# A mixture-of-experts layer: two experts' products summed in PSUM by one set of 0/1 matmuls, in two places of a turn, and 8 KB rows of down weights

## The reference

```python
# t: 576 x 1024 (normalised tokens); 4 groups x 8 experts; gates: 2 of 32 are nonzero for a token
for g in range(N_GROUPS):
    e = slice(g * EXPERTS_PER_GROUP, (g + 1) * EXPERTS_PER_GROUP)
    hg = jnp.einsum('td,edf->tef', t, w_gate[e])       # 1024 -> 512
    hu = jnp.einsum('td,edf->tef', t, w_up[e])
    h = jax.nn.silu(hg) * hu * gates[:, g, :, None]
    y = y + jnp.einsum('tef,efd->td', h, w_down[e])    # 512 -> 1024
x = rmsnorm(x + y)
```

## Time and profile before

| | us |
|---|---|
| median of 3 runs | 769.97 |
| the three runs | 769.97, 767.77, 771.99 |
| the profiled execution | 769.66 |
| its span | 767.8 |
| PE / DVE / ACT busy | 710.1 / 400.0 / 110.3 |
| DMA, mean over the span | 299 GB/s |

### The profile page before, as it was taken

How to read it: one execution, slowest core, us unless ns; L and a number is a source line. 1 busy time by engine, 2 the same in 40 slices (tenths; PEclk the granted TensorE clock), 3 DMA queues, 4 the chain that set the end, 5 groups by cost and what they waited for, 6 DMA issues and landing times.

```text
span 767.8 us, 9080 instructions
## 1 busy us (share of the span) xinstructions
PE 710.1 (92%) x3792; PEld 356.2 (46%) x3792; DVE 400.0 (52%) x697; ACT 110.3 (14%) x202; POOL 39.5 (5%) x47
## 2 busy tenths in 40 slices
PE   7999999999889999999999999999999999999691
PEld 5999999778644333333333333333333333332220
DVE  5464166424354555545555455554555545555447
ACT  6322242203200000000000000000000000000004
POOL 1000000000020001000010000000000000000000
PEclk9999999999788999999999999999999999999997
DMA  9921400583576999999999999999999999996003
GB/s 289 322 89 47 175 1 1 222 337 128 187 312 241 391 399 399 402 402 387 409 408 402 399 409 405 410 398 404 382 407 411 410 396 398 404 415 251 1 0 124
DMA packets 53421, 229.84 MB, mean 299 GB/s; under 512 B 7844, under 2 KB 15029, under 8 KB 36995
## 3 DMA queue, kind: packets, MB, share of 16 engines
q1 hardware_dynamic: 50819, 224.52, 74.8%
q0 software_dynamic: 2560, 4.73, 1.6%
HBM read 228.03 MB, written 4.85 MB: 303 GB/s over the span
## 4 chain that ended last, share of the span: by engine, by line
PE 79%; DVE 14%; ACT 3%; DMA 2%; issue 1%; SPq 1%; DVEq 0%; POOLq 0%
PE ps L1447 31%; PE ps L1467 15%; PE ps L1284 12%; PE ps L1477 8%; PE ps L1355 7%; DVE x_sb L788 6%; DVE xT L1125 2%; DVE hexp L788 2%; ACT silu_g L750 2%; DVE hexT L1133 1%; DMA x_sb<-in_x_prompt 1%; PE ps L1381 1%; DMA xg<-hn_rows,idx 1%; PE ps L1248 1%; PE ps L1250 1%
## 5 line engine op out<-in xcount | busy, mean ns | idle before, releaser
L788 DVE TENSOR_TENSOR x_sb<-ps,x_sb 128x512 f32<-128x512 f32 (+1 forms) x330 | 211.5, 682 | 136.1 <-PE ps L1477 103.3
L1447 PE MATMUL ps<-w,xT 128*64 128x512 f32 x1024 | 246.6, 605 | 1.2 <-DVE xT L1125 1.2
L1467 PE MATMUL ps<-wd,hexT 128*64 128x512 f32 x512 | 118.3, 605 | 24.9 <-DVE hexT L1133 24.9
L1447 PEld LDWEIGHTS ps<-w,xT 128*64 128x64 f32 x1024 | 65.7, 137 | 130.5 <-issue 127.6
L1477 PE MATMUL ps<-y_hi,home 64*128 64x512 f32 (+1 forms) x320 | 78.0, 484 | 8.7 <-DVE x_sb L788 5.6
L1467 PEld LDWEIGHTS ps<-wd,hexT 128*64 128x64 f32 x512 | 34.3, 138 | 95.7 <-issue 55.8
L794 DVE SCALAR_TENSOR_TENSOR y_lo<-ps,gate_of,y_hi 128x512 fp32r<-128x512 f32 x32 | 24.0, 751 | 94.7 <-ACT y_hi L754 94.7
L1477 PEld LDWEIGHTS ps<-y_hi,home 64*128 64x128 f32 (+1 forms) x320 | 28.1, 172 | 97.6 <-DVE x_sb L788 57.7
L1477 PE MATMUL ps<-y_lo,home 64*128 64x512 f32 (+1 forms) x320 | 63.5, 393 | 0.0
L750 ACT ACTIVATE silu_g<-ps 128x256 f32<-128x256 f32 x32 | 12.3, 383 | 297.8 <-PE ps L1447 297.8
L558 POOL DMA_INDIRECT xg<-hn_rows,idx x32 | 32.2, 1007 | 429.0 <-PE ps L1437 424.4
(11 more groups left out here) (205 smaller groups left out, 586.7 us busy)
## 6 DMA issues: line engine op xcount, KB each, us to landing
w<-in_moe_w_gate SPq DMA_DIRECT2D x64, 1024.0 KB, 8.3
w<-in_moe_w_up SPq DMA_DIRECT2D x64, 1024.0 KB, 10.7
wd<-in_moe_w_down SPq DMA_DIRECT2D x64, 1024.0 KB, 8.6
wo<-in_w_out SPq DMA_DIRECT2D x2, 2048.0 KB, 10.8
x_sb<-in_x_prompt SPq DMA_DIRECT2D x4, 512.0 KB, 9.1
hn_rows<-hn2p SPq DMA_DIRECT2D x4, 512.0 KB, 2.8
out<-x_sb SPq DMA_DIRECT2D x4, 512.0 KB, 2.6
wi_v<-in_w_in SPq DMA_DIRECT2D x4, 384.0 KB, 8.2
```

Of the source, the lines that this page charges most:

```text
L788: return nc.vector.tensor_tensor(out, a, b, op)
L1447: last = mm(ps[64 * h:64 * h + 64, 1, :], lhs, w1[s][:, :, k, h * (F // 2):(h + 1) * (F // 2)], start=(k == 0), stop=(k == KD - 1))
L1467: last = mm(ps[64 * h:64 * h + 64, 3, :], lhs, wd[s][:, c, h * 512:(h + 1) * 512], start=(c == 0), stop=(c == F // P - 1))
```

## The change

It has four parts.

1. **Pairs.** The homes of experts 2p and 2p+1 are one set: five homes for two experts, each of which sums y_hi and y_lo of both in PSUM (8 matmuls instead of 4), and five adds for two experts instead of ten. A third set of y_hi, y_lo and home takes the room of a routing table.
2. **Places.** `gate_up` is no longer broken up. Pair p's homes stand in turns 2p+2 and 2p+3: homes 0 and 1 after `transpose_x` and home 2 after `transpose_act` of the even turn, homes 3 and 4 after `transpose_x` of the odd turn. VectorE copies hexT ahead of xT. The last pair's homes, after turn 31, have four pairs of banks in place of two.
3. **Overflow.** Nothing is flushed ahead of `blocks_past`: turn 30's `transpose_x` and `work` are in turn 29, and its own xT stays where it is if blocks follow (they use `xT_past`).
4. **Down rows.** The rows of the down weights are dealt to partitions in twos, 8 KB of DRAM each; the transposes of the activation take every second column so that they match. SyncE issues the down weights of slot 2 when the first gather has landed, and not when it is issued.

TensorE's list, before: the `down` of turn 27 and most of turn 28's `gate_up`. L1467 is `down`, L1447 `gate_up`, L1477 the homes; x4 is four alike in a row.

The hexT copy stands behind one add, as before, and no longer behind the xT copy. The core of the diff:

```diff
             gate_v = w_gate[0].rearrange("e (p k) f -> p e (k f)", p=P)
             up_v = w_up[0].rearrange("e (p k) f -> p e (k f)", p=P)
-            down_v = w_down[0].rearrange("e (c p) d -> p e c d", p=P)
+            down_v = w_down[0].rearrange("e (h p r) d -> p e h (r d)", p=P, r=2)
             def load_down(e, s, landed=None):
                 for half in range(2):
-                    c = slice(half * (F // P // 2), (half + 1) * (F // P // 2))
-                    sp.dma_start(wd[s][:, c, :].rearrange("p (o c) d -> p o c d", o=1),
-                                 down_v[:, bass.ds(e, 1), c, :]).then_inc(landed or wd_in[s], 16)
+                    sp.dma_start(wd[s][:, 2 * half:2 * half + 2, :].rearrange("p (o c) d -> p o (c d)", o=1),
+                                 down_v[:, bass.ds(e, 1), half, :]).then_inc(landed or wd_in[s], 16)
...
-            sp.wait_ge(idc_seen, 2)
+            sp.wait_ge(xg_in[0], 16)
             load_down(2, 2)
...
-                pool.sem_inc(idc_seen, 1)
                 gather(xg[:, s, :], idx[:, n:n + 1], xg_in[s])
...
-            def turn(n, adds, more=True):
-                if adds:
-                    for j in range(3):
-                        add_first(n - 1, j)
+            def turn(n):
+
+                p, second = n // 2 - 1, n % 2
                 work_h(main, n)
-                if more:
+                if p >= 0:
+                    add_pair(p, 3 * second)
+                work_hT(main, n)
+                if n < NE - 1:
                     work(main, n + 1)
-                if adds:
-                    add_first(n - 1, 3)
-                work_hT(main, n)
-                if adds:
-                    add_first(n - 1, 4)
+                if p >= 0:
+                    for j in ((1, 2), (4,))[second]:
+                        add_pair(p, j)
...
-                    last = nc.tensor.transpose(ps[:, 2, c * P:(c + 1) * P], hexp[:, c * P:(c + 1) * P], ident)
+                    last = nc.tensor.transpose(ps[:, 2, c * P:(c + 1) * P], hexp[:, c:F // 2:2], ident)
...
+                steps = [(buf, y) for buf in bufs for y in (y_hi, y_lo)]
+                for i, (buf, y) in enumerate(steps):
                     for h in range(2):
                         r = slice(64 * h, 64 * h + 64)
+                        last = mm(ps[0:n, bank + h, :], home[buf][r, t], y[buf][r, :], start=(i == 0),
+                                  stop=(i == len(steps) - 1))
                 last.then_inc(S["home_ps"], 1)
 
-            def home_first(n, j):
-                turn = n * NT + j
+            def home_pair(p, j):
+                q = p * NT + j
                 if j == 0:
-                    pe.wait_ge(main["lo_ready"], n + 1)
-                if turn >= 2:
-                    pe.wait_ge(main["added"], turn - 1)
-                send_home(main, n % 2, j, turn)
-
-            def turn(n, homes, more=True):
+                    pe.wait_ge(main["lo_ready"], 2 * p + 2)
+                if q >= 2:
+                    seen = q - 1 if p < NPAIR - 1 else min(q - 1, p * NT) if j < 4 else p * NT + 1
+                    pe.wait_ge(main["added"], seen)
+                send_home(main, (2 * p % 3, (2 * p + 1) % 3), j, LAST_BANKS[j] if p == NPAIR - 1 else bank_of(q))
+
...
-                gate_up(main, n, s, w1_in[s], need, between)
-                if more:
+                gate_up(main, n, s, w1_in[s], need)
+                if n < NE - 1:
                     transpose_x(main, (n + 1) % NSLOT, xg_in[(n + 1) % NSLOT], 16 * ((n + 1) // NSLOT + 1))
-                if homes:
-                    home_first(n - 1, 3)
+                if p >= 0:
+                    for j in ((0, 1), (3, 4))[second]:
+                        home_pair(p, j)
                 transpose_act(main, n)
-                if homes:
-                    home_first(n - 1, 4)
+                if p >= 0 and not second:
+                    home_pair(p, 2)
...
             transpose_x(main, 0, xg_in[0], 16)
             stay_warm(WARM[3], x_sb[:, 0, :])
             for n in range(LAST):
-                turn(n, n > 0, n < LAST - 1)
-            for j in range(NT):
-                home_first(LAST - 1, j)
+                turn(n)
...
             blocks_past(pe, before_past, block_past, after_past)
-            transpose_x(main, LAST % NSLOT, xg_in[LAST % NSLOT], 16 * (LAST // NSLOT + 1))
             for n in range(LAST, NE):
-                turn(n, n > LAST, n < NE - 1)
+                turn(n)
             for j in range(NT):
-                home_first(NE - 1, j)
+                home_pair(NPAIR - 1, j)
```

More of the change, by code:

```diff
@@ L265, in build @@
     back = region(routing_at, where["zp"])
-    y_hi = back("y_hi", [P, 2, D // 2], F32R)
-    y_lo = back("y_lo", [P, 2, D // 2], F32R)
-    home = back("home", [P, 2, T], F32R)
+    y_hi = [back(f"y_hi{b}", [P, D // 2], F32R) for b in range(2)]
+    y_lo = [back(f"y_lo{b}", [P, D // 2], F32R) for b in range(2)]
+    home = [back(f"home{b}", [P, T], F32R) for b in range(2)]
     p1 = region(where["zp"], pool_end)
@@ L285, in build @@
     onehot_p = p3("onehot_p", [P, 3, NT * 2, NOV], F32R)
+    third = region(where["onehot_s"], pool_end)
+    y_hi.append(third("y_hi2", [P, D // 2], F32R))
+    y_lo.append(third("y_lo2", [P, D // 2], F32R))
+    home.append(third("home2", [P, T], F32R))
+    xT_past = nc.alloc_sbuf_tensor_at("xT_past", [P, KD // 2, P], F32, offset=where["xg"])
     choices = memb[:].rearrange("p t k e -> p (t k) e")
@@ L753, in high @@
                 act.wait_ge(S["dn_ps"], done)
-                nc.scalar.activation(y_hi[:, buf, :], ps[:, 3, :], ACT.Copy, scale=gate).then_inc(S["hi_ready"], 1)
+                nc.scalar.activation(y_hi[buf][:], ps[:, 3, :], ACT.Copy, scale=gate).then_inc(S["hi_ready"], 1)
             def block_first(n):
@@ L1135, in low, with add @@
             def low(S, n, buf, row, gate):
-                ts(home[:, buf, :], row_ids[:], row, None, ALU.is_equal)
+                ts(home[buf][:], row_ids[:], row, None, ALU.is_equal)
                 dve.wait_ge(S["hi_ready"], n + 1)
-                stt(y_lo[:, buf, :], ps[:, 3, :], gate, y_hi[:, buf, :].bitcast(F32), ALU.mult,
+                stt(y_lo[buf][:], ps[:, 3, :], gate, y_hi[buf][:].bitcast(F32), ALU.mult,
                     ALU.subtract).then_inc(S["lo_ready"], 1)
-            def add(S, n, j, turn, seen):
+            def add(S, j, bank, seen):
                 m = TOK[j]
@@ L1206, in _ @@
             for j in range(NT):
[L1207 removed]
+                add_pair(NPAIR - 1, j)
                 if j:
@@ L1438, in transpose_x, with gate_up @@
                 last.then_inc(S["xT_ps"], 1)
-            def gate_up(S, n, s, landed, need, between=nothing):
+            def gate_up(S, n, s, landed, need, xT=xT):
                 pe.wait_ge(S["xT_ready"], n + 1)
@@ L1452, in gate_up @@
                         last.then_inc(S["gu_ps"], 1)
-                    between(k)
             def transpose_act(S, n):
@@ L1469, in down, with send_home @@
                 last.then_inc(S["dn_ps"], 1)
-            def send_home(S, buf, j, turn):
+            def send_home(S, bufs, j, bank):
                 n, t = TOK[j], slice(j * P, j * P + TOK[j])
-                for part, y in enumerate((y_hi, y_lo)):
+                steps = [(buf, y) for buf in bufs for y in (y_hi, y_lo)]
+                for i, (buf, y) in enumerate(steps):
                     for h in range(2):
                         r = slice(64 * h, 64 * h + 64)
-                        last = mm(ps[0:n, 4 + 2 * (turn % 2) + h, :], home[r, buf, t], y[r, buf, :], start=(part == 0),
-                                  stop=(part == 1))
+                        last = mm(ps[0:n, bank + h, :], home[buf][r, t], y[buf][r, :], start=(i == 0),
+                                  stop=(i == len(steps) - 1))
@@ L1512, in _ @@
             for n in range(LAST):
-                turn(n, n > 0, n < LAST - 1)
-            for j in range(NT):
-                home_first(LAST - 1, j)
+                turn(n)
             def before_past():
                 pe.sem_inc(spill["dn_ps"], 1)
-                pe.wait_ge(main["added"], LAST * NT)
+                pe.wait_ge(main["added"], (LAST // 2 - 1) * NT)
+                pe.wait_ge(main["xT_ready"], LAST + 1)
+                pe.wait_ge(main["lo_ready"], LAST)
             def block_past(b):
                 transpose_x(spill, SPARE, xg_past, 16 * b + 16)
-                gate_up(spill, b, SPARE, w1_past, 32 * b + 32)
+                gate_up(spill, b, SPARE, w1_past, 32 * b + 32, xT_past)
                 transpose_act(spill, b)
```

50 lines of the change are left out of this document (24 added, 26 removed).

## The result

| | before | after |
|---|---|---|
| median, us | 770.74 (4 runs) | 711.46 (4 runs) |
| the runs, us | 767.77 to 771.99 | 709.0 to 715.88 |
| the profiled execution, its span | 769.66, 767.8 | 710.51, 708.5 |

The ratio of the times is 0.9242, with a 95% interval of 0.9188 to 0.9297. The change makes the kernel 7.6% faster; 716 us was forecast, with a range of 706 to 730.

What follows compares the result with a forecast made beforehand. TensorE's order was taken to bound the experts, the weight stream shortly behind. The later of two paths, TensorE's 713.1 and the stream's 708.8, plus 1 us for late pieces gave 714.1 of span; forecast 716 us, range 706 to 730.

Steps and rivals of the forecast that it cites:

- the crossing: The weight stream starts two turns ahead, loses 0.9 us a turn and meets TensorE only in the last turns.
- late pieces: 1 us added to the span for weight pieces that come late where TensorE's path and the stream's cross.
- The turns: TensorE's expert turns: even ones take 14.84 us and odd ones 14.14, against 16.03 before.
- The flush: Homes ahead of the overflow test and the restart cost 8.46 us before turn 30; gain 8, with 0.5 left for the test.
- The start: First gather without down weights beside it: gain between nothing and 1.8 us, taken as 1.0; turn 1 starts at 246.0.
- The stream's path: Weight pieces at 2.50 us, 15.35 a turn with the gather, end the span at 708.8 us.
- The rows of the down weights: Down rows of 8 KB instead of 4 KB: no gain counted; a 5% slower 4 KB piece would make 7 us.
- The strided read: Activation's two transposes: nothing taken, covered by the add in odd turns; in even ones 0.44 in 15 turns, 7 us.
- Turn 30 and the tail: End of the experts: turn 30, now with homes, gives back 2.4 us and the tail 0.5.
- The stream decides at 2.56 a piece: Rival: at 2.56 us or more a piece the weight stream sets the end, 720 to 730 us; chance 0.18.
- Homes dearer: Rival: home steps in their new places cost 0.335 us each, 20 us over 29 turns, giving 736 us; chance 0.10.
- The clock falls: Rival: waits for weights lower TensorE's clock in the second half of gate_up, giving 816 us; slower by the clock, chance 0.02.

Runs made afterwards that it cites:

- the kernel without homes: The changed kernel with the homes and adds of all pairs but the last left out: 708.69 us, ratio 0.9184.
- The kernel without homes and with 4 KB rows: The changed kernel with homes and adds of all pairs but the last left out and down weights in 4 KB rows: 713.80 us, ratio 0.9254.
- the odd turn's 6 us: The changed kernel with home 4 behind transpose_act and hexT copied ahead of home 3's add in odd turns: 710.72 us, ratio 0.9219.

## Why the prediction was right

The beat, the places of the waits and the crossing came out as worked out; the time was 4.5 us too high, of 5.6 in the span. The 5.6 are 2.6 at the start of turn 1, 2.0 in turns 2 to 29, 0.5 for the overflow test and 1.0 set aside for late pieces, less 0.5 for turns 30 and 31, which took longer. Point by point:

- *The turns.* 14.84 and 14.14 were forecast, 14.75 and 14.10 measured. Over turns 2 to 29 that is 2.0 us. `gate_up` unbroken is 6.96 (270.48 to the `transpose_x` at 277.44) and not 7.02; the rest is right within 0.03. An even turn is 0.65 longer than an odd one, 0.70 by the forecast. But I called this the price of the wait of home 2 for home 0's add, and that was a wrong name for it: the wait is less than 0.1, as the transposes of the activation end with the add, and the price is home 2's own 1.13 ahead of `down` less the 0.52 of an odd turn's wait for hexT. The sum had these terms right.
- *The flush* went with no gap left; the 0.5 for the overflow test was not needed. Undoing it alone costs 5.5, the 9.3 of the flush less what two turns without homes give back.
- *The start* is the term that was mis-sized most. "The gain is between nothing and 1.8 ... I take 1.0." It was 3.7. The bound was wrong: I took 5.3, the landing of a piece of 1 MB, as the least that a gather could take. The gathers issued in 216 to 220.6 in the kernel after answer:

```profile
DMA to landing us min/median/max: 3.1/3.4/3.7
```

  A gather moves 0.15 MB and should not have been bounded by a piece seven times its size. What held TensorE then is the routing's matmuls, not the gather. Undoing the edit costs 4.3 in the time.
- *The stream's path.* Forecast 708.8 of span, measured 707.5 in the kernel without homes. That near hit is two errors that cancel: the stream started 2.7 earlier than I had it, at 243.46, and a turn took 15.46 in place of 15.35, 3.1 over 28 turns. Of the 1.7 that is left, 0.9 is turn 31, which has no homes in that kernel; 0.8 stays open.
- *The rows of the down weights.* "I count nothing and leave both to the range" was the one step that failed by its reasoning. I wrote that a slower 4 KB piece would be "7 us of a path that doesn't decide". Rows of 4 KB cost 3% of a piece, 4.3 us of the stream's path, and this is enough for it to decide: 3.3 us of the time. The mean of a burst of mixed pieces over 15 us could not show 3%.
- *The strided read* costs 0.07 in a turn whose hexT copy waits for the transposes (14.10 against 14.03 with rows of 4 KB), and nothing in the even turn. I had it the other way round: home 2 covers it in the even turn, and in the odd turn the add ends just ahead of the transposes and covers all but this.
- *Turn 30 and the tail.* Turn 30 took 15.2 (14.84 forecast), with the first wait for weights in it. The tail gave back the 0.5 that was forecast.

The rivals. *The stream decides at 2.56 a piece:* it did not; by the turns of 15.46, less 0.35 for a gather, a piece takes 2.52 with 8 KB rows, and by those of 15.61 a mean one 2.54 with 4 KB down rows, which already push the time up. I wrote that the Trainium skill speaks against the change. Its 408.7 GB/s ("DMA: Bandwidth & Descriptors", section "SWDGE vs HWDGE vs iDMA") is given for rows of 4 KiB. The change takes the down weights, the only ones in such rows, out of them, so the figure does not speak against it. Nor does it fall in this case: by a piece of 2.50 + 0.077 an estimate for a stream of 4 KB rows here is 407 GB/s, while 8 KB rows move 419 to 420. *Homes dearer:* a step behind another takes 0.23 in the new places too. *The clock falls:* from turn 1 to the end of the experts the kernel after is granted 1.00. But the mechanism exists. Ahead of turn 1 the kernel after shows

```profile
235.00:240.00 5.00, 5.00 (x18) 3.23 (x20) 0.98 (x4) 0.00 (x0) 0.00 (x0) 0.52 0.97 402
```

Before this TensorE had waited 0.56 and then run the 30 small matmuls of the routing, so here a low clock follows no wait of 4.5; `down` of turn 0 takes 5.80 in place of 3.65. The kernel without homes waited in each turn from about turn 12 on, and once, at a wait of 2.54, its timeline reads

```profile
535.14 3.65 PE L1455 MATMUL ps<-w,xT 128*64 128x512 f32 x16 [0.93 <-DMA w<-in_moe_w_up]
541.33 5.35 PE L1455 MATMUL ps<-w,xT 128*64 128x512 f32 x16 [2.54 <-DMA w<-in_moe_w_up]
```

and the window of these 5 us:

```profile
540.00:545.00 5.00, 3.67 (x12) 1.21 (x14) 0.00 (x0) 0.00 (x0) 0.00 (x0) 0.77 1.01 421
```

That half of `gate_up` took 1.70 more. Among its 38 waits for weights it was the only one (the kernel without homes and with 4 KB rows shows one as well), so at 2 in 100 this rival was not priced too low by that count.

## What to carry to other kernels

When a faster engine meets a stream that is nearly full, price both paths to the end and find the turn in which they cross. A gain on the first path behind the crossing is worth nothing (the odd turn's 6 us gave none), and a small cost of the second suddenly counts (3% on a third of the pieces was 3.3 us). Bound a transfer by rows of its own size. And side work between the matmuls of a tuned loop is cheapest in one block, in a gap that exists anyway: a home cost 1.28 in `gate_up`, of which 1.03 was its own work, and 0.78 in the changed kernel ((14.43 - 12.48) / 2.5), where it fills time in which TensorE would wait.

## What I had not expected of the hardware

An issue on a queue that is 27 us deep holds up its issuer; I read this as a full queue. These are answers on the weights of gate and up in 300 to 400 and in 500 to 600 us, kernel after (count, duration in ns as min/median/max, first and last start, then times to landing):

```profile
L473 SPq DMA_DIRECT2D w<-in_moe_w_up x14: 432/433/845, 303.3 to 393.4; - x14
DMA to landing us min/median/max: 13.1/17.9/23.3
```

```profile
L473 SPq DMA_DIRECT2D w<-in_moe_w_up x12: 2127/2175/2442, 507.6 to 591.3; - x12
DMA to landing us min/median/max: 26.0/27.4/28.6
```

Pieces queue for longer and longer until the 11th or so, 27 us deep (27.4 / 2.50). From there an issue takes 2.1 us and more in place of 0.43, about the time of a piece. The chain that ended last shows these issues as SPq from 530 to 637, 15% of the span, although in all that time TensorE does not wait for weights, and in turn 30 only 0.24 us; a reader could take them for the bound. The gathers are on another queue and do not get slower as this one fills: they land in 6.7 us in 300 to 400 and in 6.9 in 560 to 660.
